# The seam between the second perceptron and the difference attention, by token halves

## What is computed

```python
h_lat = h_lat + ga2 * squared_relu_mlp(
    modulate(rms_norm(h_lat, g_mlp[i]), sh2, sc2), mlp_w1[i], mlp_w2[i])
...
def squared_relu_mlp(h, w1, w2):
    return jnp.square(jax.nn.relu(h @ w1)) @ w2
...
# second block: p = rmsnorm(x, l0_pre_g_2) @ w_in, of which the first
# columns are da_q, da_k, da_v; the rest of the mixer follows
def rmsnorm(x, g):
    xf = x.astype(jnp.float32)
    y = xf * lax.rsqrt(jnp.mean(xf * xf, axis=-1, keepdims=True) + EPS)
    return (y * g.astype(jnp.float32)).astype(x.dtype)
```

## Time and profile before

| | before |
|---|---|
| time, median of 3 executions | 2734.12 us (2729.07 to 2738.08) |
| the profiled execution, time | 2735.49 us |
| its span | 2733.7 us |
| TensorE busy (share of the span) | 2619.9 us (96%) |
| VectorE busy | 1549.0 us (57%) |
| ScalarE busy | 1072.7 us (39%) |
| GpSimd busy | 875.9 us (32%) |
| mean granted TensorE clock | 0.992 of full speed |

### The profile page before, as it was taken

The page is one execution under the profiler, slowest core; times in us unless marked ns, Lnnn a source line. Parts: engine busy times, 40 slices in busy tenths (PEclk is TensorE's granted clock), DMA queues, the critical chain, the costliest instruction groups (busy, mean ns, idle before and its releaser), DMA issues. The chain is left out here.

```text
span 2733.7 us, 38265 instructions
## 1 busy us (share of the span) xinstructions
PE 2619.9 (96%) x14748; PEld 2129.2 (78%) x14748; DVE 1549.0 (57%) x2903; ACT 1072.7 (39%) x1864; POOL 875.9 (32%) x651
## 2 busy tenths in 40 slices
PE   6899999999999999999899999999999999999997
PEld 4787786788888888766668888787778888788886
DVE  5434444687777778555664444544556445516555
ACT  4444544422222223565542322354553434542222
POOL 1211121243333333021124444333334333444443
PEclk9999999999999999999999999999999999999999
DMA  6323333223333332110012222322213221222221
GB/s 246 114 86 96 113 101 101 85 104 106 106 105 106 106 107 72 52 47 32 32 47 95 105 92 92 96 64 76 77 48 102 69 86 62 94 93 93 93 93 62
DMA packets 69652, 243.02 MB, mean 89 GB/s; under 512 B 11780, under 2 KB 29700, under 8 KB 49288
## 3 DMA queue, kind: packets, MB, share of 16 engines
q1 hardware_dynamic: 69512, 241.15, 26.3%
HBM read 239.02 MB, written 2.10 MB: 88 GB/s over the span
## 5 line engine op out<-in xcount | busy, mean ns | idle before, releaser
L248 POOL TENSOR_TENSOR w_lo<-w_raw,w_hi 128x512 fp32r<-128x512 f32 x612 | 820.8, 1373 | 1737.3 <-ACT w_hi L241 604.9
L287 PE MATMUL bank<-u_hi,w_hi 128*128 128x512 f32 (+1 forms) x1952 | 732.3, 375 | 10.8 <-DVE u_lo L548 5.0
L289 PE MATMUL bank<-u_hi,w_lo 128*128 128x512 f32 (+1 forms) x1952 | 719.6, 369 | 0.0
L288 PE MATMUL bank<-u_lo,w_hi 128*128 128x512 f32 (+1 forms) x1952 | 718.7, 368 | 0.0
L287 PEld LDWEIGHTS bank<-u_hi,w_hi 128*128 128x128 f32 x1952 | 368.6, 189 | 82.0 <-issue 10.7
L288 PEld LDWEIGHTS bank<-u_lo,w_hi 128*128 128x128 f32 x1952 | 368.8, 189 | 62.1 <-issue 2.5
L289 PEld LDWEIGHTS bank<-u_hi,w_lo 128*128 128x128 f32 x1952 | 368.4, 189 | 62.5
L1088 DVE SCALAR_TENSOR_TENSOR resid<-bank,mod,resid 128x512 f32<-128x512 f32 (+1 forms) x384 | 242.1, 658 | 141.2 <-PE bank L289 136.4
L287 PE MATMUL bank<-hid_hi,w_hi 128*128 128x512 f32 (+1 forms) x768 | 275.5, 359 | 0.0
L289 PE MATMUL bank<-hid_hi,w_lo 128*128 128x512 f32 (+1 forms) x768 | 273.0, 355 | 0.0
L288 PE MATMUL bank<-hid_lo,w_hi 128*128 128x512 f32 (+1 forms) x768 | 272.1, 354 | 0.0
(11 more groups left out here) (411 smaller groups left out, 3885.3 us busy)
## 6 DMA issues: line engine op xcount, KB each, us to landing
w_raw<-stream SPq DMA_DIRECT2D x150, 1024.0 KB, 4.9
w_raw<-stream SPq DMA_DIRECT2D x56, 512.0 KB, 4.5
ada_ring<-stream SPq DMA_DIRECT2D x48, 512.0 KB, 4.7
bias<-bias SPq DMA_DIRECT2D x192, 64.0 KB, 2.3
ada_more<-stream SPq DMA_DIRECT2D x6, 1024.0 KB, 12.4
resid<-h SPq DMA_DIRECT2D x2, 1536.0 KB, 9.2
w_raw<-stream SPq DMA_DIRECT2D x8, 256.0 KB, 3.9
out<-resid SPq DMA_DIRECT2D x8, 256.0 KB, 2.0
```

The lines of the kernel that those rows point to most:

```text
L248: ins = eng.tensor_tensor(m.wl[:, s, w], m.raw[:, s, w], m.wh[:, s, w].bitcast(F32), ALU.subtract)
L287: pe.matmul(out, lh, rh, start=start, stop=False)
L288: pe.matmul(out, lh, rl, start=False, stop=False)
L289: return pe.matmul(out, ll, rh, start=False, stop=stop)
```

## The change

In the second layer's perceptron block w is computed as two blocks of 256 tokens, p and q, with the same weights. The first half goes to even, the second to odd PSUM banks. The squares, the sum, the reciprocal root, the scaling and splitting and the first projection run per half (`half_stats`, `HalfApply`). TensorE sums half 0 behind the third tile of q and half 1 behind the third tile of the projection of half 0. Three of the eight scales of each half (`HELPED`) go to GpSimd, without the gain, which ScalarE and VectorE then apply. The low part of chunk 0 moves from VectorE to GpSimd, two quarters between the adds of half 0 and two behind them; the low part of chunk 1 moves to GpSimd, behind all its scales. The high part of chunk 1 stands on ScalarE behind the reciprocal root of half 1. VectorE's list has the evictions of p, those of q, then scales and low parts of half 0, then of half 1, with three scales ahead of the first low part.

The two stages share one block, so the meeting of the engines between them is gone, and so are the filler products on both sides of it. SP's list of `diff_stage` begins with a wait for the last product of q; its first two loads wait for the low parts of chunks 0 and 1. TensorE's projection waits for the low part of chunk 0, its values for that of chunk 1. The first layer's perceptron keeps its order.

```diff
--- before.py
+++ after.py
@@ -393,6 +396,12 @@
...
+
+
+def half_stats(m):
+
+    return [Stats(m, (m.h[:, c, LAT:TOK], m.h[:, 2 + c, LAT:TOK]), m.h[:, 4 + c, LAT:TOK], m.h[:, 6 + c, LAT:TOK])
+            for c in range(2)]
@@ -558,6 +567,82 @@
...
+class HalfApply:
...
+
+    def __init__(self, m, stats, added, gain, shift, tmp, helped=()):
+        self.m, self.stats, self.added, self.gain, self.shift, self.tmp = m, stats, added, gain, shift, tmp
+        self.helped = helped
...
+    def scale(self, eng, n):
+        c, k, t = self.tokens(n)
+        if n >= len(self.tmp):
+            eng.wait_ge(*self.low.at(n - len(self.tmp) + 1))
+        eng.wait_ge(*self.added(k, c))
+        eng.wait_ge(*self.stats[c].rooted())
+        if n in self.helped:
+            eng.tensor_tensor(self.place(n), self.m.h[:, k, t], self.stats[c].rstd, ALU.mult).then_inc(self.pooled.sem)
+        else:
+            eng.scalar_tensor_tensor(out=self.place(n), in0=self.m.h[:, k, t], scalar=self.gain(k),
+                                     in1=self.stats[c].rstd, op0=ALU.mult, op1=ALU.mult).then_inc(self.scaled.sem)
+
+    def hi(self, act, n):
+        c, k, t = self.tokens(n)
+        if n in self.helped:
+            act.wait_ge(*self.pooled.at(self.helped.index(n) + 1))
+            ins = act.activation(self.m.uh[:, k, t], self.place(n), ACT.Copy, scale=self.gain(k))
+            ins.then_inc(self.high.sem)
+            return
+        act.wait_ge(*self.scaled.at(n + 1 - sum(x < n for x in self.helped)))
+        if self.shift is None:
+            ins = act.activation(self.m.uh[:, k, t], self.place(n), ACT.Copy)
...
+        ins.then_inc(self.high.sem)
...
+    def lo(self, dve, n):
+        c, k, t = self.tokens(n)
+        m, high = self.m, self.m.uh[:, k, t].bitcast(F32)
+        dve.wait_ge(*self.high.at(n + 1))
+        if n in self.helped:
+            ins = dve.scalar_tensor_tensor(out=m.ul[:, k, t], in0=self.place(n), scalar=self.gain(k), in1=high,
+                                           op0=ALU.mult, op1=ALU.subtract)
...
+            ins = dve.tensor_tensor(m.ul[:, k, t], self.place(n), high, ALU.subtract)
...
+        ins.then_inc(self.low.sem)
...
+    def dve(self, dve, first, last, ahead):
+
+        mine = [n for n in range(first, last) if n not in self.helped]
+        for n in mine[0:ahead]:
+            self.scale(dve, n)
+        for n in range(first, last):
+            for x in mine[ahead:ahead + 1]:
+                self.scale(dve, x)
+            mine = mine[:ahead] + mine[ahead + 1:]
+            self.lo(dve, n)
@@ -829,7 +914,11 @@
...
-def mlp_stage(nc, m, layer, tok, rstd, first, second):
+HALF = dict(p=0, q=1)
+HELPED = [5, 6, 7, KT + 5, KT + 6, KT + 7]
+
+
+def mlp_stage(nc, m, layer, tok, rstd, first, second, gain=None):
@@ -845,7 +934,10 @@
...
         else:
-            after = late_stats(m)
+            after = half_stats(m)
+            spare = relu[:, :, :, :].rearrange("p a t n -> p (a t) n")
+            entry = HalfApply(m, after, lambda k, c: (D.sem, D.at(f"e_{'pq'[c]}{k}")), gain, None,
+                              [spare[:, n // 2, n % 2 * (tok // 2):(n % 2 + 1) * (tok // 2)] for n in range(8)], HELPED)
...
-        with nc.Block() as block:
+        for block in (m.block,):
@@ -971,16 +1064,52 @@
                 split_hi(act, m, 4 * rounds + 3, 4, None)
                 act.wait_ge(E.sem, E.at(f"v{KT - 1}"))
                 coming.high(act, 0)
+                if layer == 0:
...
+                def square_of(c, k):
+                    act.wait_ge(*entry.added(k, c))
+                    after[c].square(act, k, m.h[:, k, c * half:c * half + half])
                 for k in range(KT):
-                    act.wait_ge(D.sem, D.at(f"e_w{k}"))
-                    after.square(act, k, m.h[:, k, :] if layer == 0 else quarters(m.h[:, k, 0:LAT]))
+                    square_of(0, k)
+                for k in range(4):
+                    square_of(1, k)
+                after[0].root(act, m.bank[:, 4, 0:half])
+                square_of(1, 4)
+                square_of(1, 5)
+                entry.hi(act, 0)
+                square_of(1, 6)
+                entry.hi(act, 1)
+                square_of(1, 7)
+                for n in range(2, KT):
+                    entry.hi(act, n)
+                after[1].root(act, m.bank[:, 6, 0:half])
+                act.wait_ge(E.sem, E.at(f"q{KT - 1}"))
                 coming.high(act, 1)
-                after.root(act, m.lin[1][:, 0:tok] if layer == 0 else quarters(m.lin[1][:, 0:tok]))
+                for n in range(KT, 2 * KT):
+                    entry.hi(act, n)
...
             def _(pool):
                 split_lo_loop(pool, m, 8, [CHUNK] * 4, last=True)
-                after.add(pool)
+                if layer == 0:
+                    after.add(pool)
+                    return
+                for k in range(1, 6):
+                    after[0].add_one(pool, k)
+                    if k in (2, 4):
+                        coming.low_quarter(pool, 0, k // 2 - 1)
+                coming.low_quarter(pool, 0, 2)
+                coming.low_quarter(pool, 0, 3)
+                after[1].add(pool)
+                for n in HELPED:
+                    entry.scale(pool, n)
+                coming.low(pool, 1)
@@ -1032,12 +1161,16 @@
...
-                        for a, b, _ in spans(tok):
+                        for a, b, _ in spans(tok) if g not in HALF else [(HALF[g] * half, HALF[g] * half + half, 0)]:
+                            o_ = place(g, n)[:, a:b] if g not in HALF else m.bank[:, 2 * (n % 4) + HALF[g], 0:half]
                             for k in range(2):
-                                last = mm3(pe, place(g, n)[:, a:b], wh[:, k, n * P:n * P + P],
+                                last = mm3(pe, o_, wh[:, k, n * P:n * P + P],
                                            wl[:, k, n * P:n * P + P], hid_h[:, par, k, a:b],
                                            hid_l[:, par, k, a:b], k == 0, k == 1)
                         last.then_inc(*E.mark(f"{g}{n}"))
+                        if g == "q" and n == 2:
+                            pe.wait_ge(D.sem, D.at(f"e_p{KT - 1}"))
+                            after[0].sum(pe, [(m.bank[:, 4, 0:half], lambda t: t)])
@@ -1058,10 +1191,15 @@
...
+                if layer:
+                    down_("p", 1, 4 * rounds + 3, 1, [("lo_d1", (z,))],
+                          lambda n: [(D, f"e_v{n + 4}", ())] if n < 4 else [(D, f"e_p{n - 4}", ())])
+                    down_("q", 1, 4 * rounds + 3, 1, [], lambda n: [] if n < 4 else [(D, f"e_q{n - 4}", ())])
+                    pe.wait_ge(D.sem, D.at("e_q4"))
+                    return
                 down_("w", 1, 4 * rounds + 3, 1, [("lo_d1", (z,))],
                       lambda n: [(D, f"e_v{n + 4}", ())] if n < 4 else [(D, f"e_w{n - 4}", ())])
-                after.sum(pe, [(m.lin[1][:, a:b], (lambda t, a=a, b=b: t[:, a:b]) if layer == 0 else (lambda t: t))
...
                 keep_busy(pe, m, m.lin[3][:, 0:LAT], 2)
...
+                def down_half(g):
+                    c = HALF[g]
+                    t = slice(c * half, c * half + half)
+                    for n in range(KT):
+                        dve.wait_ge(E.sem, E.at(f"{g}{n}"))
+                        own(dve, D)
+                        dve.scalar_tensor_tensor(out=m.h[:, n, t], in0=m.bank[:, 2 * (n % 4) + c, 0:half],
+                                                 scalar=m.mod[:, layer, 5, n, 0:1], in1=m.h[:, n, t], op0=ALU.mult,
+                                                 op1=ALU.add).then_inc(*D.mark(f"e_{g}{n}"))
@@ -1146,6 +1294,12 @@
...
+                if layer:
+                    down_half("p")
+                    down_half("q")
+                    entry.dve(dve, 0, KT, 3)
+                    entry.dve(dve, KT, 2 * KT, 3)
+                    return
...
                 coming.low(dve, 1)
+        if layer:
+            m.tail = E.sem, E.at(f"q{KT - 1}")
     finish_stage(m, 32)
-    return after
+    return after if layer == 0 else (entry, coming)
@@ -2660,8 +2816,6 @@
...
-        norm = Apply(m, rstd_u, LAT, lambda k, w: col(m, "pre0")[:, k:k + 1], None,
-                     [t[:, n, :] for t in (z, gate) for n in range(2)])
...
             def _(sp):
                 def load(f):
                     n, (kind, j) = fill[f], f
                     s = n % 2
-                    if n >= 4:
-                        sp.wait_ge(*chunk_lo.at(n - 3))
+                    sp.wait_ge(*(chunk_lo.at(n - 3) if n >= 4 else loaded.lo.at(n - 1)))
...
+                sp.wait_ge(*m.tail)
                 sp.dma_start(causal[:, :], m.in_cst[:, CST["causal"][0]:CST["causal"][1]]).then_inc(causal_in.sem, 16)
                 for f in fills[2:]:
                     load(f)
...
-                norm.act(act)
...
-                norm.dve(dve)
@@ -3031,14 +3183,19 @@
...
-                    for k in range(KT):
-                        pe.wait_ge(*norm.ready(k))
```

(76 more changed lines are left out.)

14 lines of the change are left out of this document (10 added, 4 removed).

## The result

The changed kernel takes 2740.23 us in the median (2739.16 to 2744.7); the kernel before took 2734.12. The ratio is 1.0032, with a 95% interval of 1.0022 to 1.0042, so the change costs 8.7 us (6.0 to 11.5): slower, by about as much as this kernel's measurement can tell. The forecast was 2740.3 us. That the medians meet so well is partly luck, as the stretch shows.

The account below looks back on a forecast made before the run. TensorE's order of time was taken as the bound, 96% busy outside the seam. The stretch grows 5.0 us and one clock fall adds 1.2: 2734.12 + 6.2 = 2740.3 us, range 2731.5 to 2745.

Parts of the forecast that it names:

- Steps 1 to 4: Block p to the projection of half 0: TensorE waits 1.65 and 4.3 us, projection starts 1.9 earlier, work until 1771.05.
- Step 5: Norm of half 1: VectorE passes one instruction per GpSimd instruction, low parts done 1773.1 to 1777.3, TensorE until 1781.8.
- Steps 5 and 6: Norm of half 1, TensorE until 1781.8; then 3.8 us of filler and the block's end removed, not a gain of their own.
- the sum without the clock: Block w's first product to the values' first: end at 1781.8 + 0.1 against 1776.91, 5.0 us longer.
- The clock term: TensorE's clock falls once, after the 4.3 us idle piece before the projection: 1.2 us, bounds nothing and 3.6.
- The rival with several falls: Two or three full falls of TensorE's clock: +7.4 to +8.6, 2741.5 to 2742.7 us; chance 0.10.
- The split-pays rival: VectorE and GpSimd pass each other better at 256 columns, or pieces fit VectorE's gaps: 2732.7 to 2734 us; chance 0.15.
- the chain with VectorE undisturbed: The same steps without GpSimd delaying VectorE: end at 1775.4, 1.4 us shorter than before.
- Dearer GpSimd: GpSimd's 256-column instruction costs much more than 0.74, beyond the noise from 0.88; at 0.92, +8.7, 2742.8 us; chance 0.13.
- No overlap of the halves: Sum of half 1 also waits for GpSimd: TensorE stands some 2 us more, 2742.3 us; chance 0.05.
- time outside the stretch: Sign of being wrong: time moves outside the span from block w's first product to the values' first product.
- step 7: SP's next load waits until the values' weights are split, 1777.0; there by 1783, some 5 later, covered by 12 us.

Follow-up runs that it names:

- kernel with filler: Changed kernel plus filler products in TensorE's waits: four before the projection, two and one before tiles 0 and 1 of half 1; stretch 37.95 us, time 1.0025.
- the kernel without the six scales: Changed kernel with GpSimd's six scales back on VectorE, the low part of the values' weights left with GpSimd; stretch 36.4 us.

## Why the prediction was right, and where it was not

All times here count from the first product of the last block. The changed kernel with filler stands beside, since its clock does not fall.

| step | forecast | after | with filler |
|---|---|---|---|
| 2: sum of half 0 begins | 9.55 | 9.3 | 9.3 |
| 3: projection begins | 18.95 | 18.9 | 18.9 |
| 4: sum of half 1 begins | 21.2 | 22.3 | 21.2 |
| 5: first low part of half 1 is done | 28.2 | 30.9 | 29.35 |
| 5: tile 1 of half 1 begins | 31.05 | 33.7 | 32.2 |
| values begin | 37.0 (38.2 with the clock) | 40.7 | 37.95 |

**Steps 1 to 4** held to 0.3 us where the clock stays up (last column); in the changed kernel step 4 is 1.1 late by the clock alone. GpSimd's 256-column instruction, extrapolated at 0.72 and taken at 0.74, measures 0.72 alone and 0.83 to 0.88 in the mean where VectorE passes between (2.50 and 2.64 us for three scales); the loss of 0.16 per VectorE instruction was right. That TensorE's projection would start only 1.9 us earlier, because VectorE has all evictions first and then blocked scales, is what the trace shows. The idle pieces of 1.65 and 4.3 us were 1.39 and 4.52.

**Step 5** was right in kind (one VectorE instruction per GpSimd piece, each blocked one 1.4 us behind the last, two waits of TensorE for u_lo, though of 3.19 and 1.18 us and not of 2.1 and 2.0) and off by one instruction. It lets three scales of half 1 pass before the first low part; VectorE's list has four, and the fourth meets GpSimd's first piece of 512. The four take 4.22 us where the step left 3.1, from 1768.6 to 1771.7. About half of that comes back because GpSimd is done before low part 2. **Steps 5 and 6 left out a wait**: the values' first bank is free only when ScalarE has copied the queries. In the kernel before these were finished three products of 512 ahead of the end, now only three of 256, and TensorE stands 0.42 us. Together the sum without the clock, 5.0, is 5.95 in the kernel with filler.

**The clock term was mis-sized.** I took one fall for 1.2 us, within bounds of 0 and 3.6; the filler experiment measures 2.8. The first fall, which I priced at 1.2, cost about 1.5. The rival with several falls is what happened: one behind the 4.5 us wait and a longer one that shows behind the 3.2 us wait, over tiles 0 to 2 of half 1, where I had put nothing and it cost 1.3. My reason against it, that VectorE limits there, fails from tile 1 on, where the low parts are ready faster than the slow products use them.

So the stretch cost 8.7 us, not 6.2, on the border of what counts as slower by over 0.3%, for which I gave 0.2. The forecast time met the median because the two medians happened to differ by 6.1 us; the rest of the span varies by more between executions than the 2.5 us that my sum fell short. The range held the time either way. The split-pays rival is out: VectorE and GpSimd do not pass each other better at 256 columns. The split alone, once GpSimd and the clock are taken out of it, is worth 0.8 us, where the chain with VectorE undisturbed had 1.4. Dearer GpSimd is out by the 0.72. No overlap of the halves is half true: half 0's norm waits for all of q in VectorE's list.

Of the signs named for being right, the values' start some 37 us after block p missed, at 40.7. Of those for being wrong, time outside the stretch is the one left open: the 1.4 us behind it are in both executions of the changed kernel and in neither of the kernel before, and the prediction had nothing for them.

The load behind the values' weights, step 7, was sent at 1772.95 and cost nothing, as forecast. One reading of the earlier trace rows was narrow: L2936 there reads a single tensor and a scalar per partition, not two tensors, and is blocked all the same.

## What to carry to other kernels

Before moving elementwise work from VectorE to GpSimd, look at what VectorE does at that moment: its instructions with both operands in SBUF each waited for the whole GpSimd instruction in flight here, and six helped scales plus one moved chunk cost 6.75 us where they were to save some 5 us of VectorE time. If it must be so, cut GpSimd's work into short instructions where another engine waits for VectorE's first results; VectorE's last results come no sooner by it. When filler products are removed from a seam, first ask whether the waits they covered are gone; the clock that falls costs on the products that follow, not in the wait. And where a kernel varies by more than the change, measure the change in a stretch between two fixed points of the trace: it repeated to 0.1 us while the rest of the span moved by 6.5. Look at the granted clock in it before comparing two kernels, and at the time behind it as well.

## What the runs showed of the hardware

- A VectorE instruction of 256 columns with two SBUF operands: 0.41 alone, 0.94, 1.48 and 2.56 us beside GpSimd pieces of 256, 512 and 1024 columns. GpSimd loses about 0.15 us per VectorE instruction that passes, not the whole of it. The Trainium skill, page "SBUF — State Buffer", section "Who interferes with whom", calls the ports that the two share an exclusive lock, by which whichever engine comes second fully blocks. The traces agree for VectorE. For GpSimd they show less than a full block; how much of one its own start-up covers, no run here separates.
- The evictions, with one operand in PSUM and one in SBUF, stayed at 0.48 us beside GpSimd's adds and low parts, as this one in the changed kernel:

```profile
1743.97 0.48 DVE L1243 SCALAR_TENSOR_TENSOR resid<-bank,mod,resid 128x256 f32<-128x256 f32 x1 [0.22 <-PE bank L289]
1743.93 1.29 POOL L486 TENSOR_TENSOR w_lo<-w_raw,w_hi 128x512 fp32r<-128x512 f32 x1
```

- Two full operands in SBUF are not the only case: a `tensor_scalar` of 256 columns (L2936 of the kernel before), with one tensor and a scalar per partition, took 0.34 us at 1821.03, where GpSimd stood still, and 1.27 at 1793.67 beside a low part.
- GpSimd's piece alone: 0.72 us for 256 columns, 1.28 for 512. For 1024 columns no piece ran alone: two took 5.00 with two VectorE instructions between.
- TensorE's clock fell to 1.2 GHz during or just after idle pieces of 4.5, 3.2, 3.6 (pieces of 1024 columns) and, in the kernel with all norm work on VectorE, 3.05 us. After the same 3.05 us in the kernel without the six scales it stayed at 2.4 GHz and fell only behind two later waits of 1.86 and 0.78 us. So a wait of 3 us by itself did not decide it. With filler and idle pieces of up to 1.6 us between it stayed at 2.4 GHz.
